# Splitting a weight slot in two halves, each given back by the TensorE on its own

## The reference, cut to what matters

```python
for l in range(DEPTH):                      # first block; the second is alike, with swiglu
    mod = cond @ w_mod[l] + b_mod[l]
    h = rms_norm(x, norm_g[l, 0]) * (1.0 + sc1) + sh1
    y = mixer_block(h, ...)                 # h @ w_in, the mixers, @ w_o
    x = x + gt1 * rms_norm(y, norm_g[l, 1])
    h = rms_norm(x, norm_g[l, 2]) * (1.0 + sc2) + sh2
    y = jnp.square(jax.nn.relu(h @ w_up[l])) @ w_down[l]
    x = x + gt2 * rms_norm(y, norm_g[l, 3])
```

## Time and profile before

| what | value |
|---|---|
| median of three runs | 1763.88 us (1752.91 to 1769.57) |
| the profiled execution's own time | 1753.19 us |
| its span, first to last instruction | 1751.3 us |
| TensorE busy | 1551.9 us, 89% |
| VectorE busy | 1071.8 us, 61% |
| ScalarE busy | 716.3 us, 41% |
| granted TensorE clock, mean | 0.918 of full |

### The profile page before, as it was taken

How to read it: one execution, slowest core, us unless ns; L and a number is a source line. 1 busy time by engine, 2 the same in 40 slices (tenths; PEclk the granted TensorE clock), 3 DMA queues, 4 the chain that set the end, 5 groups by cost and what they waited for, 6 DMA issues and landing times. The chain is left out here.

```text
span 1751.3 us, 27370 instructions
## 1 busy us (share of the span) xinstructions
PE 1551.9 (89%) x11950; PEld 1498.5 (86%) x11950; DVE 1071.8 (61%) x1279; ACT 716.3 (41%) x797; POOL 281.6 (16%) x221
## 2 busy tenths in 40 slices
PE   2887679999898689999897685999998998899999
PEld 2886679999787589999897583999998997899998
DVE  6766758687465548688474643576536764456444
ACT  2534345534452445533574411433334443343332
POOL 0000200043000001044000111010034910300012
PEclk9998779999799679999898785899998999999999
DMA  9670549888141228888252000377654773336550
GB/s 395 228 264 1 192 183 343 304 335 314 72 145 49 90 79 336 315 322 327 102 187 96 1 1 26 139 293 276 253 193 168 289 277 132 144 134 228 217 208 34
DMA packets 47207, 336.71 MB, mean 192 GB/s; under 512 B 5360, under 2 KB 5744, under 8 KB 6768
## 3 DMA queue, kind: packets, MB, share of 16 engines
q1 hardware_dynamic: 46224, 333.09, 51.1%
q10 hardware_dynamic: 864, 1.87, 0.3%
HBM read 333.89 MB, written 1.05 MB: 191 GB/s over the span
## 5 line engine op out<-in xcount | busy, mean ns | idle before, releaser
L417 DVE TENSOR_TENSOR weights_hi_lo<-ring,weights_hi_lo 128x2048 fp32r<-128x2048 f32 x213 | 511.0, 2401 | 399.6 <-ACT weights_hi_lo L411 398.6
L411 ACT ACTIVATE weights_hi_lo<-ring 128x2048 fp32r<-128x2048 f32 x213 | 407.5, 1915 | 634.0 <-PE PS L519 348.3
L519 PE MATMUL PS<-hi,weights_hi_lo 128*128 128x256 f32 x3200 | 525.9, 287 | 25.4 <-DVE weights_hi_lo L417 16.9
L519 PEld LDWEIGHTS PS<-hi,weights_hi_lo 128*128 128x128 f32 x3200 | 450.6, 195 | 29.1 <-DVE weights_hi_lo L417 18.8
L789 PE MATMUL PS<-acts_hi_lo,weights_hi_lo 128*128 128x256 f32 x3552 | 439.4, 286 | 29.5 <-DVE weights_hi_lo L417 16.4
L789 PEld LDWEIGHTS PS<-acts_hi_lo,weights_hi_lo 128*128 128x128 f32 x3552 | 433.1, 193 | 36.1 <-DVE weights_hi_lo L417 20.0
L519 PE MATMUL PS<-lo,weights_hi_lo 128*128 128x256 f32 x1600 | 326.7, 286 | 0.0
L519 PEld LDWEIGHTS PS<-lo,weights_hi_lo 128*128 128x128 f32 x1600 | 253.7, 195 | 0.0
L428 DVE CUSTOM_DVE_ANT_0 ring<-ring,cond 128x1024 f32<-128x1024 f32 x192 | 247.6, 1328 | 0.5 <-DMA smallS<-in_small_dram 0.5
L737 POOL CAST acts_hi_lo<-arena 128x512 fp32r<-128x512 f32 x74 | 67.7, 914 | 978.0 <-PE PS L789 545.6
L519 PE MATMUL PS<-weights_hi_lo,hi 128*128 128x256 f32 x1248 | 204.9, 286 | 9.2 <-DVE weights_hi_lo L417 8.0
(11 more groups left out here) (325 smaller groups left out, 1112.6 us busy)
## 6 DMA issues: line engine op xcount, KB each, us to landing
ring<-in_stream_dram SPq DMA_DIRECT2D x313, 1024.0 KB, 5.0
constS<-in_const_dram SPq DMA_DIRECT2D x1, 1856.0 KB, 11.1
cond<-in_rows_dram SPq DMA_DIRECT2D x2, 512.0 KB, 5.7
arena<-in_x_dram ACTq DMA_DIRECT2D x1, 1024.0 KB, 12.0
smallS<-in_small_dram SPq DMA_DIRECT2D x1, 883.0 KB, 12.7
out_dram<-arena ACTq DMA_DIRECT2D x2, 256.0 KB, 2.5
out_dram<-arena SPq DMA_DIRECT2D x2, 256.0 KB, 2.8
constS<-in_const_dram SPq DMA_DIRECT2D x1, 320.0 KB, 13.2
```

The lines of the kernel that those rows point to most:

```text
L411: act.activation(wsp[:, g % 2, 0, :], ring[:, n % RING, :], ACT.Copy).then_inc(*hi_ready.one())
L417: dve.tensor_tensor(wsp[:, g % 2, 1, :], ring[:, n % RING, :], wsp[:, g % 2, 0, :].bitcast(F32), ALU.subtract).then_inc(used["dve"], 1)
L519: mm = pe.matmul(o, lhs, rhs, start=k + g + j == 0, stop=k == KD - 1 and j == 2, skip_group_check=True)
```

## The change

Each split is done in two halves of 1024 columns (`HALF`), with semaphores of their own. TensorE gives each half of the buffer back by itself, and waits for each half by itself. For column products a half is four of the eight k; for row products it is one of the two row tiles g, and so that TensorE is done with a half at the middle, row products now run over g outside and k inside, except the last product of a phase, which keeps its order and waits for both halves at its start. The first half's release in that last product comes at its last k. Some semaphore names that are used nowhere are dropped too.

```diff
+HALF = SLOT // 2
...
+        half_multiplied, half_hi_ready, half_lo_ready = sig("half_slot_multiplied"), sig("half_hi_ready"), sig("half_lo_ready")
...
         def split_hi(act, n):
             wait_slot(act, n)
             g = product_no[n]
-            if g >= 2:
-
-                act.wait_ge(multiplied.sem, g - 1)
-            act.activation(wsp[:, g % 2, 0, :], ring[:, n % RING, :], ACT.Copy).then_inc(*hi_ready.one())
+            for half, at, released, ready in ((0, 0, half_multiplied, half_hi_ready), (1, HALF, multiplied, hi_ready)):
+                if g >= 2:
+
+                    act.wait_ge(released.sem, g - 1)
+                act.activation(wsp[:, g % 2, 0, at:at + HALF], ring[:, n % RING, at:at + HALF], ACT.Copy).then_inc(*ready.one())
         def split_lo(dve, n):
             g = product_no[n]
-            dve.wait_ge(hi_ready.sem, g + 1)
-            dve.tensor_tensor(wsp[:, g % 2, 1, :], ring[:, n % RING, :], wsp[:, g % 2, 0, :].bitcast(F32),
-                              ALU.subtract).then_inc(used["dve"], 1)
+            for half, at, ready, done in ((0, 0, half_hi_ready, (half_lo_ready.sem, 1)), (1, HALF, hi_ready, (used["dve"], 1))):
+                dve.wait_ge(ready.sem, g + 1)
+                dve.tensor_tensor(wsp[:, g % 2, 1, at:at + HALF], ring[:, n % RING, at:at + HALF],
+                                  wsp[:, g % 2, 0, at:at + HALF].bitcast(F32), ALU.subtract).then_inc(*done)
...
                 for i, n in enumerate(gemm):
-
-                    pe.wait_ge(used["dve"], ordinal[n][1])
...
                     for k in range(KD):
+                        if k == 0:
+                            pe.wait_ge(half_lo_ready.sem, product_no[n] + 1)
+                        if k == KD // 2:
+                            mm.then_inc(*half_multiplied.one())
+                            pe.wait_ge(used["dve"], ordinal[n][1])
...
                 for i, n in enumerate(slots):
-
-                    pe.wait_ge(used["dve"], ordinal[n][1])
                     w_hi, w_lo = halves_of(n, "rows")
...
+                    pe.wait_ge(half_lo_ready.sem, product_no[n] + 1)
+                    if i == last:
+
+                        pe.wait_ge(used["dve"], ordinal[n][1])
-                    for k in range(KD):
-                        if before and i == 0 and k == KD - 1:
+                    for g, k in sorted(((g, k) for g in range(2) for k in range(KD)), key=lambda o: o[::-1] if i == last else o):
+                        if before and i + g == 0 and k == KD - 1:
...
-                        for g in range(2):
-                            for j, (w, x) in enumerate(pieces(w_hi, w_lo, a_hi, a_lo)):
-                                mm = pe.matmul(y_of(k), w[:, g, k * P:(k + 1) * P], x[:, g, :],
+                        if i < last and g == 1 and k == 0:
+                            mm.then_inc(*half_multiplied.one())
+                            pe.wait_ge(used["dve"], ordinal[n][1])
+                        for j, (w, x) in enumerate(pieces(w_hi, w_lo, a_hi, a_lo)):
+                            mm = pe.matmul(y_of(k), w[:, g, k * P:(k + 1) * P], x[:, g, :],
...
-                        if i == last and k in unit_ends:
+                        if i == last and g == 0 and k == KD - 1:
+                            mm.then_inc(*half_multiplied.one())
+                        if i == last and g == 1 and k in unit_ends:
```

More of the change, by code:

```diff
@@ L1203, in nsa_phase @@
             cs, sd, ex, pc = sig("cmp_scores"), sig("cmp_shifted"), sig("cmp_exp"), sig("cmp_probs")
-            pct, pcs, oc, oct_ = (sig(n) for n in ("cmp_probs_T", "cmp_probs_T_taken", "cmp_out", "cmp_out_taken"))
-            ws, wt, mxd, pe_, ptp, pts, ob, obt = (sig(n) for n in (
-                "scores_in_psum", "scores_taken", "row_max", "probs_ready", "probs_T_in_psum", "probs_T_taken",
-                "attn_out", "attn_out_taken"))
+            pct, pcs, oc = (sig(n) for n in ("cmp_probs_T", "cmp_probs_T_taken", "cmp_out"))
+            ws, wt, mxd, pe_, ptp, pts, ob = (sig(n) for n in (
+                "scores_in_psum", "scores_taken", "row_max", "probs_ready", "probs_T_in_psum", "probs_T_taken", "attn_out"))
             gd, fin, ft = sig("gates_ready"), sig("outputs_ready"), sig("outputs_turned")
@@ L1619, in delta_inputs @@
             taken = sig("gemm_bank_taken")
-            tap0, cv, sl, sqd, ss, rt, nr = (sig(n) for n in (
-                "first_tap", "conv_done", "conv_silu", "squares_ready", "l2_sums", "root_ready", "l2_done"))
+            tap0, cv, sl, sqd, ss, rt = (sig(n) for n in (
+                "first_tap", "conv_done", "conv_silu", "squares_ready", "l2_sums", "root_ready"))
             ga, ge, gl, bt = sig("gate_abs"), sig("gate_exp"), sig("gate_log"), sig("beta_ready")
```

6 lines of the change are left out of this document (3 added, 3 removed).

## The result

| what | before | after |
|---|---|---|
| median of the runs | 1762.22 us (4 runs, 1752.91 to 1769.57) | 1730.3 us (4 runs, 1726.26 to 1733.97) |
| the profiled execution's own time | 1753.19 us | 1729.34 us |
| its span | 1751.3 us | 1727.3 us |
| granted clock, mean | 0.918 | 0.915 |

The ratio after to before is 0.9836, 95% interval 0.9801 to 0.9871: the change takes 1.6% off.

A forecast was written before the change was run, and what follows sets the result against it. TensorE, 89% busy, sets the time; only its stalls can be won. Terms 7.1 + 10.0 + 3.5 + 5.5 + 3.0 + 0.5 = 29.6 us take 1753.2 to 1723.6; with 10.7 to the median, 1734 us, range 1716 to 1754.

The forecast's parts named there:

- What a half costs: Splits: first half ready 2.35 us after ScalarE starts, instead of 4.28; each slot costs ScalarE 0.2, VectorE 0.15 us more.
- TensorE's own cost: Middle of each product: one more increment and wait, and the new row order, taken as 0; upper bound 23 us.
- Place 1: Second product after a normalisation: six waits for VectorE's split, 7.3 us in all, would go; gain 7.1 us.
- Place 2: Mix projections, layers 0 and 1: 10.0 of the 17.6 us waited there would be won.
- place 5: Clock drops to 1.2 GHz behind five longer waits; two of the three not otherwise counted would go: 3.0 us.
- the ring: Layer 1 mix projection: splits and side work of VectorE and ScalarE wait on each other in turn; 2.8 us won.
- rival A: Waits move instead of going, as side work or VectorE's queue becomes the bound: 1750 us; chance 0.20 together with D.
- D: VectorE takes both halves directly in succession, so TensorE gains only VectorE's 1.07 us: 1749 us; chance 0.20 with rival A.
- Place 3: Start of the out phases, layers 2 and 3, where nothing is split ahead: 1.75 us each, 3.5 us won.
- Place 4: Down phases of layers 0 and 1: steps of 5.68 us, 4.5 us won; out phase of layer 0: 1.0 us.
- rival B: Fewer stalls keep the clock at 2.4 GHz beyond the two dips counted: 1726 us, down to 1718; chance 0.14.
- Place 6: Tails in layers 2 and 3: normalisation may start when TensorE ends, not 0.15 us later, three times: 0.5 us.

The follow-up runs named there:

- toll: Changed kernel with six more increments and six more satisfied waits inside each product, last row products of a phase excepted: 1726.63 us, one execution.
- order_only: Kernel before with only the row products' new order (g outside, k inside, except the last of a phase): 1757.84 us, one execution.
- mods_early: Changed kernel with the mod slots of out and down phases one place earlier, none between the last two products: 1725.56 us, ratio 0.9791.
- whole_wait: Changed kernel, but TensorE waits for both halves before every product; halves and mid-product release stay: 1742.64 us, ratio 0.9906.
- late_release: Changed kernel, but ScalarE waits for the whole product g-2 before it writes either half: 1726.77 us, ratio 0.9825.
- after_third: Changed kernel, unedited, run again: 1729.32 us (6 runs), ratio 0.9815.

## Why the prediction was right, and where it was not

**What bounds.** Right: TensorE's stalls were what could be won, and VectorE's and ScalarE's longer busy times did not bring new ones on the whole.

**What a half costs.** The latency was right: first half 2.3 us after ScalarE's start (said 2.35). The extra of a slot was said too high only where its halves follow each other at once. Two splits in the projection of layer 1, ScalarE and then VectorE, in the timeline after:

```profile
481.63 1.99 ACT L414 ACTIVATE weights_hi_lo<-ring 128x1024 fp32r<-128x1024 f32 x2
...
487.17 1.99 ACT L414 ACTIVATE weights_hi_lo<-ring 128x1024 fp32r<-128x1024 f32 x2
```

```profile
482.71 2.36 DVE L421 TENSOR_TENSOR weights_hi_lo<-ring,weights_hi_lo 128x1024 fp32r<-128x1024 f32 x2 [2.35 <-ACT weights_hi_lo L414]
...
489.52 0.42 DVE L1044 TENSOR_TENSOR arena<-arena 128x256 f32<-128x256 f32 x1
489.86 2.35 DVE L421 TENSOR_TENSOR weights_hi_lo<-ring,weights_hi_lo 128x1024 fp32r<-128x1024 f32 x2
```

Two halves in a row take 1.99 us on ScalarE and 2.36 on VectorE, against 1.90 and 2.29 whole: 0.09 and 0.07 us more, since the second starts before the first has ended in the records. Predicted were 0.2 and 0.15, from widths measured singly, and that is what halves cost that stand apart: 1.22 us each undisturbed, 0.15 a slot over 2.29. The sum was said too low. The busy time of VectorE's split rose by 74.5 us (511.0 to 585.5; all of VectorE by 67) where 32 were said. The halves' own cost is 213 x 0.15, some 33 us, less 9 where the records overlap; the other 51 us fell beside GpSimd: of the 426 halves in the trace 103 took over 0.1 us more than an undisturbed one, 74 us in all, and all 103 ran beside an operation of GpSimd (of the other 323 only 14 did), against 34 of 213 whole splits and 23 us before. The prediction had allowed for that contention in one place only.

**TensorE's own cost.** Zero, as taken: toll's row products take 62.48 us with six more waits and increments each, and order_only's 5.68 us.

**Place 1**, second products: all six waits are gone, 7.3 us for the 7.1 said. The six phases they stand in fell by 9.9 us, of which 1.65 is the clock behind that wait in layer 3 (the step from the second product to the third is 7.28 us before and 5.63 after) and the rest mostly the step between column products, which changes from execution to execution (last section).

**Place 2**, mix projections. TensorE's waits in them, after, windows 43 to 137 and 449 to 545, against the earlier trace rows:

```profile
PE PS L526 <- DVE weights_hi_lo L421: 5.1, 2, 4.0
```

```profile
PE PS L526 <- DVE weights_hi_lo L421: 3.9, 3, 1.7
```

From 17.6 to 9.0 us, 8.6 won where 10.0 was said; the phases fell by 12.9 us. The rest goes with the clock, in place 5. One step of the working failed. It had the second product of the ring start at ScalarE's next split plus 2.35 us. ScalarE's part came true and better: the splits at 481.63 and 487.17 are 5.5 us apart instead of 8.1. But VectorE had side work until 489.9 (L1044 above), so that the first half came 4.0 us after ScalarE's start; TensorE in the timeline after, against the earlier trace rows:

```profile
484.08 0.72 PE L526 MATMUL PS<-weights_hi_lo,hi 128*128 128x256 f32 x4 [1.08 <-DVE weights_hi_lo L421]
...
491.22 0.71 PE L526 MATMUL PS<-hi,weights_hi_lo 128*128 128x256 f32 x4 [1.14 <-DVE weights_hi_lo L421]
```

The two starts stand 7.14 us apart, against 8.06 before and 6.65 forecast. "What is late next: VectorE's own queue of side work" named it and priced it at nothing. This is what rivals A and D said of such places; it held in this one and not as a whole.

**Place 3**, out phases of layers 2 and 3. In the timeline after, against the earlier trace rows:

```profile
1072.04 3.90 ACT L414 ACTIVATE weights_hi_lo<-ring 128x1024 fp32r<-128x1024 f32 x4 [7.46 <-PEq L1774]
1073.13 6.79 DVE L421 TENSOR_TENSOR weights_hi_lo<-ring,weights_hi_lo 128x1024 fp32r<-128x1024 f32 x4 [1.72 <-ACT weights_hi_lo L414]
...
1075.17 5.08 PE L800 MATMUL PS<-acts_hi_lo,weights_hi_lo 128*128 128x256 f32 x27 [4.55 <-DVE weights_hi_lo L421]
```

TensorE starts 3.1 us after ScalarE, 1.5 us sooner than before (the waits fell from 6.06 to 4.55, and alike in layer 3): 3.0 where 3.5 was said. The first half was ready 3.1 us after ScalarE's start and not 2.35 + 0.5, since it took 0.3 us more beside GpSimd's operation than was allowed.

**Place 4**, down phases of the mix layers: 3.6 us for 4.5. The steps of 5.68 us came as forecast (two of 5.75 in layer 0 apart), and rival A falls on them. What is left of the excess, 0.8 and 0.7 us, is the last product, which waits for both halves behind the last mod slot. For the down phases the prediction did not look at that product; for the out phase of layer 0 it did, gave it 1.0 us of gain "from VectorE's lead", and that failed: the wait there is 3.2 us (2.8 before), and 3.7 in another execution. VectorE has no lead in that phase; the last product starts 22.4 us after the phase's first matmul, 22.3 before, and moving the mod slots (mods_early) only moved the wait. There rival A holds. The reason given for the steps, "from 1.4 to about 6.2 us of slack" by the release at mid product, is enough by itself, as whole_wait shows (95.00 and 94.79 us), but the prediction did not see that it isn't needed: late_release has only 3.4 us of slack and the start on the first half, and takes 95.08 and 94.98.

**Place 5**, the clock. Windows (PE, PEld, DVE, ACT, POOL busy, PEclk, DMA share, GB/s), after: the stretch that answers to 1334 to 1338 of before, and the two mix projections; behind them the same projections before.

```profile
1315.40:1319.40 4.00, 4.00 (x37) 4.00 (x35) 4.00 (x5) 1.22 (x2) 3.84 (x3) 1.00 0.97 410
...
43.00:130.00 87.00, 81.65 (x628) 79.01 (x629) 68.29 (x115) 43.69 (x60) 5.23 (x6) 0.98 0.65 252
449.00:534.00 85.00, 81.01 (x632) 78.33 (x633) 49.72 (x81) 45.97 (x62) 4.25 (x6) 0.97 0.38 137
```

```profile
43.00:137.00 94.00, 83.73 (x631) 80.57 (x632) 67.30 (x105) 42.27 (x49) 3.23 (x6) 0.96 0.63 233
451.00:542.00 91.00, 82.98 (x625) 80.25 (x626) 48.38 (x70) 44.90 (x51) 3.17 (x6) 0.93 0.35 128
```

The mean clock rises from 0.96 and 0.93 to 0.98 and 0.97, and TensorE's busy time, for the same matmuls, falls by 2.1 and 2.0 us. So of the 12.9 - 8.6 = 4.3 us of these phases that are not waits, nearly all goes with the clock. With 1.65 at the second product of layer 3, the clock behind removed stalls gave back 5.9 us in this pair of executions; 3.0 was the term, so it was undersized, on rival B's side. How much it gives is not the same in each execution: in after_third the two projections take 88.48 and 86.21 us, 2.9 more than here, and order_only, with whole splits, had no such fall in the projection of layer 3 but one of the same size in its last up phase (a step of 7.29 us).

**Place 6**, tails: 1.3 us in the three stretches, for 0.5.

**Sum and median.** The forecast for the profiled execution was 1723.6 us; it took 1729.3. The 5.7 us are nearly all one stretch that the prediction did not touch, TensorE's 48 matmuls in the attention of layer 0 (a row by source for before, then after; 275 and 421 ns each, and the windows over them, with PEclk):

```profile
L1394 PE MATMUL PS<-arena x48: 275/275/294, 175.1 to 180.4; 128*128 128x64 f32 x48
...
175.00:181.00 6.00, 5.54 (x48) 5.43 (x48) 1.03 (x6) 0.00 (x0) 0.00 (x0) 1.00 0.00 0
```

```profile
L1406 PE MATMUL PS<-arena x48: 421/421/443, 168.8 to 178.8; 128*128 128x64 f32 x48
...
169.00:179.00 10.00, 10.00 (x48) 10.00 (x48) 0.01 (x1) 0.00 (x0) 0.00 (x0) 0.50 0.00 0
```

Before, they ran at 2.4 GHz; after, at 1.2, and took 10.4 us instead of 5.5. It is not the change alone that does it: order_only, with the old splits, has this stretch at 66.61 us and 421 ns, while the changed kernel has it at 62.97 in after_third, and toll at 62.99 and 275 ns. Over all the traces the matmuls ran at the lower clock in 7 of 11 with split slots and in 1 of 2 with whole ones; whether the change makes it more frequent can't be told from so few. In the 19 us ahead of it TensorE was busy for 15 us at a mean clock of 0.73 to 0.78 in both kernels. The Trainium skill (TensorE: Matmul & The Clock Gate, Part 1: The HAM clock gate) says that the number of matmuls that run at the lower level before the clock rises differs from run to run of the same kernel; these executions agree, with 5 us between them. On the other side, the 10.7 us that lay between the profiled execution and the median were carried over whole, and the changed kernel's profiled execution lies only 1.0 us under its median. The profile of before was the luckier one (it is at the low end of its runs), and such luck belongs to one execution and is no constant to add. The two errors, 5.7 too low and 9.7 too high, leave 1730.3 against 1734: that the median came this close is in part luck. The drop of 29.6 us that was summed is borne out better by the medians of all runs (31.9 us) than by this pair of profiles (23.9).

**The signs.** Waits 41 to 22.5 us, not to 12 to 16: the mix projections and the two out phases' starts hold 9.0 and 8.8 of them, and the last products of three phases, 4.7, had been left out. The first halves at the two out phases were ready 3.1 us after ScalarE's start (2.4 to 2.9 said). Means of 1.40 us for L421 (1.25 to 1.35 said) and 1.06 for L414 (as said). The clock's mean fell by 0.003 rather than rising, by the attention stretch.

## What to carry to other kernels

Where an engine waits at the start of a unit of work for a chain of two others, look at the time from the first engine's start to the consumer's, not at busy shares: cutting the operand in two shortens that chain by one half on each engine, while a satisfied wait and an increment on TensorE cost nothing here. The Trainium skill (Perfetto Trace Analysis, Optimizing Scalar/DVE Operations) says that breaking up instructions of engines that aren't saturated may let others go on sooner; the runs agree for halves (1.6% less), and four parts were no faster: the last product of a down phase, which needs all of them, waited 2.4 us for VectorE instead of 0.8. So look for what still needs the whole operand, and keep side work out of the queue in front of it. That helps where the engine has time to spare (the down phases, 1.1 and 0.9 us less) and not where its work fills the phase (the out phase of layer 0).

## What the runs showed of the hardware that was not expected

- The time from one column product to the next (48 matmuls of 128x128 by 256) is one of three values in the up phases, 5.63, 5.70 or 5.76 us, constant within a phase and different between phases and between executions of the same code: in the last up phase 5.70, 5.63 and 5.70 us in three executions of the changed kernel, 5.63 in order_only, 5.76 in toll. Over 22 products the ends are 2.9 us apart. What chooses it was not found. Row products have 5.68 us in every execution.
- Whether a sparse stretch of 48 matmuls runs at 2.4 or 1.2 GHz is not set by the code ahead of it alone: the stretch of 48 in the attention of layer 0 differs by 5 us between executions of the changed kernel.
- A half on VectorE beside one of GpSimd's operations took 2.3 us instead of 1.22 (timeline after, down phase of layer 0):

```profile
411.03 2.32 DVE L421 TENSOR_TENSOR weights_hi_lo<-ring,weights_hi_lo 128x1024 fp32r<-128x1024 f32 x1
```

The added 1.1 us is as long as for a whole slot before (3.37 instead of 2.29). Over all slowed operations the added time is 0.72 us on average for a half (103 of them) and 0.68 for a whole slot (34), so it did not grow with the length of VectorE's operation, and cutting one in two gave it more chances to meet GpSimd: in 24 slots both halves were slowed, and the total rose from 23 to 74 us. Most of it was hidden, since TensorE had only to wait for the first half.
